# A two-part transformer program on one core: narrow projections made wider, reversed queries, spectra during the down projection, idle transpositions and two reorders

## The reference

```python
def first_block(x, ...):
    n = rms_norm(h, norm1_g)
    mq, mk, mv, gq, gk, gv, g_low, g_out, gate_moba, gate_gla = split(n @ w_in)
    y_moba = softmax(rms(mq) @ rms(mk).T / 8 + t5_bias, causal) @ mv      # 8 heads of 64
    log_a = log_sigmoid(g_low @ gate_up + gate_bias) / 16
    y_gla = rms_norm(gla_attention(gq, gk, gv, log_a)) * silu(g_out)      # 4 heads, chunks of 64
    h = h + (sigmoid(gate_moba) * (y_moba @ w_bm) + sigmoid(gate_gla) * (y_gla @ w_bg)) @ w_out
    h = h + square(relu(rms_norm(h, norm2_g) @ w_up)) @ w_down
def even_layer(x, ...):
    a_val, a_gate, z_a, q, k, v, o, z_b, gates = split(rms_norm(x, g_pre) @ w_in)
    u = depthwise_conv_centred(a_val * sigmoid(a_gate), conv_w, conv_b)   # 31 taps
    y_a = silu(group_layer_norm(u)) * silu(z_a)
    h = mlstm(q, k, v, gates) + reversed mlstm                            # 4 heads
    y_b = sigmoid(o) * rms_norm(h, hn_g) * silu(z_b)
    return x + rms_norm(concat(y_a, y_b) @ w_out, g_post)
def odd_layer(x, ...):
    c_q, c_kv, k_r, f_in, z_c, z_d = split(rms_norm(x, g_pre) @ w_in)
    s = q_nope @ k_nope.T + rope(q_rope) @ rope(k_r).T                    # 8 heads, 128 + 64
    y_c = softmax(s / sqrt(192)) @ v * silu(z_c)
    y_d = (real(fft2(f_in)) @ w_fd) * silu(z_d)
    return x + rms_norm(concat(y_c, y_d) @ w_out, g_post)
```

## Time and profile before

| | us |
|---|---|
| median of 3 runs | 907.76 (906.8 to 912.4) |
| the profiled execution | 908.23 |
| its span | 906.4 |
| TensorE busy | 874.2 (96%) |
| DVE busy | 499.5 (55%) |
| ACT busy | 476.7 (53%) |
| POOL busy | 39.2 (4%) |

### The profile page before, as it was taken

The page is one execution under the profiler, slowest core; times in us unless marked ns, Lnnn a source line. Parts: engine busy times, 40 slices in busy tenths (PEclk is TensorE's granted clock), DMA queues, the critical chain, the costliest instruction groups (busy, mean ns, idle before and its releaser), DMA issues.

```text
span 906.4 us, 10691 instructions
## 1 busy us (share of the span) xinstructions
PE 874.2 (96%) x4015; PEld 704.5 (78%) x4015; DVE 499.5 (55%) x754; ACT 476.7 (53%) x756; POOL 39.2 (4%) x66
## 2 busy tenths in 40 slices
PE   4999999999999999999998999999999899999996
PEld 3888787788888888888885766888888697787685
DVE  4566734555676666435545434856765556555363
ACT  4547644754366555334345364338764567555451
POOL 2100000000000000810000010000000000000000
PEclk9999999999999999999977999999999999999999
DMA  5873445356456565767442414534564547265021
GB/s 178 263 223 120 133 137 140 117 167 206 160 187 191 181 186 186 182 227 252 145 152 80 142 46 161 162 94 163 187 216 154 151 148 253 71 196 164 1 93 47
DMA packets 76579, 141.92 MB, mean 157 GB/s; under 512 B 8489, under 2 KB 10836, under 8 KB 76528
## 3 DMA queue, kind: packets, MB, share of 16 engines
q1 hardware_dynamic: 72432, 134.37, 47.1%
q0 software_dynamic: 4032, 6.86, 2.5%
q10 hardware_dynamic: 64, 0.02, 0.0%
HBM read 140.12 MB, written 2.63 MB: 157 GB/s over the span
## 4 chain that ended last, share of the span: by engine, by line
PE 90%; ACT 4%; DVE 4%; issue 1%; DMA 1%; POOL 0%; DVEq 0%; ACTq 0%; POOLq 0%
PE acc L1518 25%; PE acc L1520 25%; PE acc L1519 25%; PE aux L1547 2%; PE aux L1780 2%; PE aux L1844 1%; PE aux L1969 1%; PE aux L1968 1%; ACT whi L530 1%; PE aux L1959 1%; PE aux L1903 1%; PE aux L1769 1%; DVE wlo L385 1%; DMA vec_in<-in_odd_g_q 1%; PE aux L1646 1%
## 5 line engine op out<-in xcount | busy, mean ns | idle before, releaser
L385 DVE TENSOR_TENSOR wlo<-raw,whi 128x1024 fp32r<-128x1024 f32 (+2 forms) x257 | 304.8, 1203 | 241.4 <-ACT whi L530 240.8
L530 ACT ACTIVATE whi<-raw 128x1024 fp32r<-128x1024 f32 (+2 forms) x257 | 264.9, 1045 | 259.5 <-PE acc L1520 219.6
L1518 PE MATMUL acc<-whi,a_hi 128*128 128x512 f32 (+3 forms) x720 | 284.8, 396 | 3.1 <-DVE wlo L385 1.5
L1520 PE MATMUL acc<-whi,a_lo 128*128 128x512 f32 (+3 forms) x720 | 279.6, 388 | 0.0
L1519 PE MATMUL acc<-wlo,a_hi 128*128 128x512 f32 (+3 forms) x720 | 279.4, 388 | 0.0
L1518 PEld LDWEIGHTS acc<-whi,a_hi 128*128 128x128 f32 x720 | 139.5, 194 | 35.2 <-issue 7.0
L1520 PEld LDWEIGHTS acc<-whi,a_lo 128*128 128x128 f32 x720 | 139.3, 194 | 26.8
L1519 PEld LDWEIGHTS acc<-wlo,a_hi 128*128 128x128 f32 x720 | 139.5, 194 | 26.2 <-issue 0.7
L1518 PE MATMUL acc<-whi,b_hi 128*128 128x512 f32 x234 | 92.4, 395 | 0.1
L1520 PE MATMUL acc<-whi,b_lo 128*128 128x512 f32 x234 | 91.2, 390 | 0.0
L1519 PE MATMUL acc<-wlo,b_hi 128*128 128x512 f32 x234 | 91.1, 389 | 0.0
(11 more groups left out here) (318 smaller groups left out, 765.4 us busy)
## 6 DMA issues: line engine op xcount, KB each, us to landing
raw<-in_even_w_in SPq DMA_DIRECT2D x56, 512.0 KB, 3.8
raw<-in_w_in SPq DMA_DIRECT2D x52, 512.0 KB, 4.2
raw<-in_w_up SPq DMA_DIRECT2D x32, 512.0 KB, 4.5
raw<-in_w_down SPq DMA_DIRECT2D x32, 512.0 KB, 4.5
raw<-in_even_w_out SPq DMA_DIRECT2D x16, 512.0 KB, 3.6
raw<-in_odd_w_in SPq DMA_DIRECT2D x16, 512.0 KB, 4.2
raw<-in_odd_w_out SPq DMA_DIRECT2D x12, 512.0 KB, 4.1
raw<-in_w_branch_gla SPq DMA_DIRECT2D x8, 512.0 KB, 3.4
```

The costliest lines, as they stand in the source:

```text
L385: return e.tensor_tensor(w_view(wlo[u % SPLIT], u), w_view(raw[u % RAW], u), w_view(whi[u % SPLIT], u).bitcast(F32), ALU.subtract)
L530: act.activation(w_view(whi[u % SPLIT], u), w_view(raw[u % RAW], u), ACT.Copy).then_inc(sem("hi_done"), 1)
L1518: pe.matmul(acc_of(c, t), ah[:, ts], hi[:, k], start=first, stop=False)
L1520: ins = pe.matmul(acc_of(c, t), al[:, ts], hi[:, k], start=False, stop=last)
```

## The change

1. norm1's gain is loaded by ACT into n1g_in before all else and transposed by itself; the other vectors are transposed after mq. ACT loads its table first. The one-hot's matmul moves behind mq's first unit.
2. Idle transpositions (`idle_turns`) of the identity: 10 before n1g, 14 before mq, 26 before H's first transposition of the third layer, 10 behind it.
3. Columns 3328 to 3599 of w_in are one chunk, glow, of 272 columns; gv1 keeps 256. In the same way eg has 272 and ew1 256; ACT copies eg's first 256 columns to EZB.
4. Queries are reversed within each tile of 128 when copied out, so that the bias can be read with a stride of +1 from one row; the copy of skew goes. ACT reverses back in PT; the reciprocals are reversed by a product with the matrix flip.
5. gq's and gk's transpositions stand behind the second pt bank.
6. In the o banks both heads' L1686 come first, then both heads' L1692.
7. The taps' spectra are made in dn1, two behind unit 7 and two behind unit 8, and ACT copies them there. gng and gnb are loaded after dn1.
8. The broadcasts mb stand two before eq and two in its middle.
9. KRT is two tiles of 128 rows, one with the lower half zero, one with the upper.

```diff
-        chunk("glow", w_in, 3584, 16, 8, "n1")
+        chunk("glow", w_in, 3328, 272, 8, "n1")
...
-            chunk(name, w_in, n0, 512, 8, "n1")
+            chunk(name, w_in, n0, 256 if name == "gv1" else 512, 8, "n1")
...
-            for name, n0 in [("ea0", 0), ("eg", 7168), ("eb0", 1024), ("ea1", 512), ("eb1", 1536), ("eq", 3072), ("ek", 3584),
+            for name, n0 in [("ea0", 0), ("eg", 6912), ("eb0", 1024), ("ea1", 512), ("eb1", 1536), ("eq", 3072), ("ek", 3584),
...
-                chunk(name, e_in, n0, 16 if name == "eg" else 512, 8, "en")
+                chunk(name, e_in, n0, {"eg": 272, "ew1": 256}.get(name, 512), 8, "en")
...
+            chain(pool.memset(flip[:, :], 0.0))
+            pool.affine_select(out=flip[:, :], in_=flip[:, :], compare_op=ALU.not_equal, fill=1.0, base=1 - P,
+                               pattern=[[1, P]], channel_multiplier=1).then_inc(sem("flip"), 1)
...
-            one = bass.AP(tensor=A["skew"].tensor, offset=A["skew"].offset, ap=[[512 * P, 8], [0, P - 1], [1, 384]])
-            pool.dma_start(A["skew"][:, 1:P, 0:384], one).then_inc(sem("skew_out"), 16)
-            pool.wait_ge(sem("skew_out"), 16)
...
-                src = bass.AP(tensor=A["skew"].tensor, offset=A["skew"].offset + 512 * P * a + P - 1,
-                              ap=[[511, P], [1024 * P, 4], [1, TOK]])
+                src = bass.AP(tensor=A["skew"].tensor, offset=A["skew"].offset + 512 * P * a,
+                              ap=[[1, P], [1024 * P, 4], [1, TOK]])
...
+                pool.wait_ge(sem("units_used"), CH[CI["dn1"]]["units"][-1] + 1)
                 pool.dma_start(gng[:, :], A["even_gn_g_2"][0].partition_broadcast(P)).then_inc(sem("gn_in"), 16)
...
+            act.dma_start(n1g_in[:, :], A["norm1_g"][0].rearrange("(r c) -> r c", c=P)).then_inc(sem("n1g_in"), 16)
+            use("natural_log_exp_and_others")
...
-                copy_out("glow", gl[:, t], t, scale=rms(0, t))
+                acc_wait(act, "glow", t)
+                act.activation(GV[:, t, 768:1024], acc_of("glow", t)[:, 0:256], ACT.Copy, scale=rms(0, t))
+                acc_free(act.activation(gl[:, t], acc_of("glow", t)[:, 256:272], ACT.Copy, scale=rms(0, t)), "glow")
...
-                aux_free(act.activation(flat(PT[:, 4 * i:4 * i + 4]), bank(("pt", i))[:, :], ACT.Copy), ("pt", i))
+                aux_free(act.activation(PT[:, 4 * i:4 * i + 4, ::-1],
+                                        bank(("pt", i))[:, :].rearrange("p (k q) -> p k q", k=4), ACT.Copy), ("pt", i))
...
+                pump("dn1", -5)
                 for n in range(2):
                     key = ("ws", 0, n)
...
+                pump("eg")
+                for t in range(NT):
+                    acc_wait(act, "eg", t)
+                    act.activation(EZB[:, t], acc_of("eg", t)[:, 0:256], ACT.Copy, scale=rms(2, t)
+                                   ).then_inc(sem("zb_copied"), 1)
...
-                        copy_out(f"ew{n}", ETMP[:, t], t, ACT.Silu, rms(2, t))
+                        if n == 0:
+                            copy_out("ew0", ETMP[:, t], t, ACT.Silu, rms(2, t))
+                        else:
+                            use(TABLES[ACT.Silu])
+                            act.activation(ETMP[:, t, 256:512], EZB[:, t], ACT.Silu)
+                            copy_out("ew1", ETMP[:, t, 0:256], t, ACT.Silu, rms(2, t))
...
-                aux_free(dve.tensor_copy(KRT[:, :], bank(("krT",))[:, 0:TOK]), ("krT",))
+                for p in range(2):
+                    own, other = slice(64 * p, 64 * p + 64), slice(64 - 64 * p, 128 - 64 * p)
+                    dve.memset(KRT[other, p], 0.0)
+                    ins = dve.tensor_copy(KRT[own, p], bank(("krT",))[own, 0:TOK])
+                aux_free(ins, ("krT",))
...
+            def idle_turns(b, n):
+
+                for _ in range(n):
+                    pe.transpose(b[:, 0:P], ident[:, :], ident[:, :])
...
-            pe.wait_ge(sem("vec_in"), 16 * (len(VEC_LOADS[0::2]) + 4))
-            pe.wait_ge(sem("vec_in_pool"), 16 * len(VEC_LOADS[1::2]))
-            b = take(("vec",))
-            give(pe.transpose(b[:, 0:P], vec_in[:, :], ident[:, :]), ("vec",))
+            idle_turns(acc[3], 10)
+            pe.wait_ge(sem("n1g_in"), 16)
+            b = take(("n1g",))
+            give(pe.transpose(b[:, 0:8], n1g_in[:, :], ident[0:8, 0:8]), ("n1g",))
...
+            idle_turns(acc[3], 14)
+            product("mq", 0, 1)
             pe.wait_ge(sem("t5_in"), 32)
...
-            product("mq")
+            product("mq", 1, 4)
...
-            product("dn1", 0, 15)
+            product("dn1", 0, 7)
+            if STAGES >= 2:
+                pe.wait_ge(sem("wcv_in"), 48)
+                for w in range(2):
+                    for n in range(2):
+                        b = take(("ws", w, n))
+                        give(pe.matmul(b[:, :], FW[:, w, 1::2], wcv_in[:, 512 * n:512 * n + 512], start=True, stop=True),
+                             ("ws", w, n))
+                    product("dn1", 7 + w, 8 + w)
+            product("dn1", 9, 15)
...
-                product("eq")
+                    if h % 2:
+                        product("eq", h - 1, h + 1)
...
-                pe.wait_ge(sem("h_out"), 2)
-                turn("on", range(4), cols(H))
+                def first_added(b):
+                    idle_turns(b, 26)
+                    pe.wait_ge(sem("h_out"), 2)
+
+                turn("on", range(4), cols(H), first_added)
+                idle_turns(acc_of("okv", 0), 10)
...
-                        ins = pe.matmul(b[:, o:o + TOK], QRT[rows, h // 2, P * t:P * t + P], KRT[rows, :],
+                        ins = pe.matmul(b[:, o:o + TOK], QRT[:, h // 2, P * t:P * t + P], KRT[:, h % 2],
```

More of the change, by code:

```diff
@@ L139, in split_keys @@
             return [("tr", name, j) for j in range((kts + 1) // 2)]
-        AUX = [("vec",)] + split_keys("n1", 8) + [("bias",)]
+        AUX = [("n1g",)] + split_keys("n1", 8) + [("bias",), ("vec",)]
         AUX += [("qkT", w, j) for w in range(2) for j in range(2)]
@@ L144, in program @@
         AUX += [("gz", 0), ("gz", 1)]
-        AUX += [("pt", i) for i in range(6)]
-        AUX += [("gqT", 0), ("gqT", 1), ("gkT", 0), ("gkT", 1)]
-        AUX += [("pv", 0), ("pv", 1), ("kdt", 0), ("kdt", 1), ("ga", 0), ("ga", 1)]
+        AUX += [("pt", 0), ("pt", 1), ("gqT", 0), ("gqT", 1), ("gkT", 0), ("gkT", 1)]
+        AUX += [("pt", i) for i in range(2, 6)]
+        AUX += [("prc",), ("pv", 0), ("pv", 1), ("kdt", 0), ("kdt", 1), ("ga", 0), ("ga", 1)]
         AUX += [("kv", j, i) for j in range(3) for i in range(2)]
@@ L254, in program @@
             ETMP = sb("ETMP", [P, NT, 512], c=c3)
+            gng, gnb = sb("gng", [P, D], c=c3), sb("gnb", [P, D], c=c3)
             WS = sb("WS", [P, 2, D], c=c3)
             SOB = sb("SOB", [P, NT, D], c=c3)
-            gng, gnb = sb("gng", [P, D], c=c3), sb("gnb", [P, D], c=c3)
+            EZB = sb("EZB", [P, NT, 256], c=c3)
             gates = sb("gates", [P, NT, 2, 2, 4], c=c3)
@@ L583, in _ @@
             act.wait_ge(sem("consts"), 1)
+            aux_done(act, ("n1g",))
+            split_hi("n1", range(4), lambda k: n1g[:, k:k + 1])
+            pump("mq", -3)
+            split_hi("n1", range(4, 8), lambda k: n1g[:, k:k + 1])
+            pump("mq", 0)
             for n in range(2):
                 act.wait_ge(sem(f"x_in{n}"), 16)
[L586 to L590, removed]
             norm_stats(0, lambda t: None)
@@ L621, in _ @@
                 copy_out("gk", GQK[:, 1, t], t, scale=rms(0, t))
+            aux_done(act, ("vec",))
             for j in range(2):
@@ L702, in _ @@
             pump("dn0")
+            if STAGES >= 2:
+                pump("dn1", -5)
+                for n in range(2):
+                    key = ("ws", 0, n)
+                    aux_wait(act, key)
+                    aux_free(act.activation(WS[:, 0, 512 * n:512 * n + 512], bank(key)[:, :], ACT.Copy, scale=64.0), key)
+                for n in range(2):
+                    key = ("ws", 1, n)
+                    aux_wait(act, key)
+                    for a in range(2):
+                        rows = slice(64 * a, 64 * a + 64)
+                        ins = act.activation(WS[rows, 1, 512 * n:512 * n + 512], bank(key)[rows, :], ACT.Copy,
+                                             scale=(-64.0, 64.0)[a])
+                    aux_free(ins, key)
             pump("dn1", 3)
@@ L986, in _ @@
             chain(dve.memset(rmask[:, :].rearrange("p (c e) -> p c e", e=64)[:, :, 0:1], 0.0))
-            aux_wait(dve, ("vec",))
-            aux_free(dve.tensor_copy(vec[:, :], bank(("vec",))[:, 0:P]), ("vec",))
-            split_lo("n1", range(4), lambda k: gain("norm1", k))
+            aux_wait(dve, ("n1g",))
+            aux_free(dve.tensor_copy(n1g[:, :], bank(("n1g",))[:, 0:8]), ("n1g",))
+            split_lo("n1", range(4), lambda k: n1g[:, k:k + 1])
             pump("mq", -3)
```

(23 more changed lines are left out.)

69 lines of the change are left out of this document (35 added, 34 removed).

## The result

The changed kernel takes 871.19 us, the median of four runs (869.05 to 873.07), against 907.56 for the kernel before in the same session (906.8 to 912.4). The ratio is 0.9595, with a 95% interval of 0.9555 to 0.9635. The forecast was 869.5 with a range of 864 to 879.

A forecast was written before the change was run, and what follows sets the result against it. TensorE, busy 96% of the span, was taken to bound the kernel. Its terms summed to 38.5 us off the profiled 908.2, giving 869.7; with the median 0.4 lower, it said 869.5, range 864 to 879.

The forecast's parts named there:

- the line through 512 and 320: Matmul start distances, 0.227 us at 512 columns and 0.147 at 320, continued to 0.127 at 272 and 0.120 at 256.
- The start: Up to the first QKN transposition: first product at 10.9 us, 6.8 earlier, half the clock loss kept; net gain 6.3.
- The o banks: Regrouped matmuls drop two of four stationary-width changes in each of four banks, 8 x 0.1: gain 0.8 us.
- Broadcasts in eq: Broadcasts in two pairs shorten sparse stretches, saving half clock of 1.6 us less a restart of 0.4: gain 1.0.
- The heads: KRT padded to 128 rows: 3.5 us per two heads instead of 4.9, gain 5.6.
- 0.7 less cover per head: In the heads, the softmax's way through DVE and ACT gets 0.7 less cover per head; no wait was charged.
- The PT banks: Around the probabilities: the 2.2 us wait for ACT's PT copies stays, now at gkT's bank; gain 0.
- The down projection: Down projection to convolution: 53.2 us becomes 37.2, less 4.3 for spectra moved into dn1; gain 11.7.
- Supply: Rival: ACT and DVE supply takes back 5 to 10 us of narrow-chunk savings at gv1, ew1 and eg; chance 0.18.
- Idle transpositions: Rival: at the start and after the post-norm they don't hold the clock; 5.1 us worse, 875; chance 0.10.
- Full-height loads: Rival: in the heads, 128-row weight loads don't hide, adding up to 3.5 us instead of giving 5.6; 879; chance 0.03.
- The narrow chunks: Rival: 272- and 256-column products leave the fast rate, 0.43 us per matmul instead of 0.12; 929; chance 0.02.

The follow-up runs named there:

- the last kernel: Changed kernel with gv1's first two units and go0's first unit moved into the PT waits, and the broadcasts placed one by one: 867.58 us, ratio 0.9555.
- two units moved: Changed kernel with gv1's first unit ahead of gk's transpositions and its second between the fourth and fifth PT bank: 866.65 us.
- wide chunks: Changed kernel with glow and eg at 16 columns again, gv1 and ew1 at 512: 888.24 us.

## Why the prediction was right

**The reading of the profile held.** Eight of ten terms came within 0.6, because they were counted in distances of starts from windows of one shape. 272 and 256 columns take what the line through 512 and 320 said: 48 matmuls of 272 in 6.11 (6.1 predicted), 48 of 256 in 5.84 (5.8 predicted). That the sum is off by only 0.3 is in part luck: +0.9 at the start and +0.6 at the o banks stand against -1.4 at the broadcasts and -0.4 at the heads.

**The start, 6.3 against 7.2.** The first product stood at 10.68 (predicted 10.9). The stretch from there, 34.12, is 1.4 above 144 x 0.227, where I had put 1.3 for the bias matmul, the vec transposition and the restarts. The larger error is the clock: I counted half of 1.6 as kept, since 2 us stay empty after the idle transpositions. The whole was kept, here and in nine more of the eleven profiled executions that have them; in the last kernel's it was not. No run undoes the early load of norm1's gain: that it is what brings the first product forward by 7.0 is read from the 11.1 us of waiting that are gone and from the first weight unit, behind which the first product now comes. Over the twelve profiled executions of this study the first product came between 9.96 and 11.96, 2.4 after the first unit's landing, and that landing moved between 7.57 and 9.56. Once, with two units moved, it was 2.75: the 14 idle transpositions took 2.8 us instead of 1.7 and held the first product back by 0.35.

**The o banks, 0.8 against 1.4.** The step "two of four changes go, 8 x 0.1" was mis-sized: over the whole stage 40 instructions went from 0.239 to 0.205 each. The eight changes that go each slowed both instructions of a matmul, not one: in the kernel before such a pair took 0.58 us into 64 columns and 0.63 back into 128, and 0.43 where the width stayed. Four of each make 1.4.

**Broadcasts in eq, 1.0 against -0.4.** The mechanism, shorter sparse stretches hold the clock, holds in five of ten profiled executions, then with 1.2 gained, which is the 1.6 - 0.4 of the prediction's own two sizes, where it wrote 1.0. In four half clock comes inside eq, behind the first pair or the second, where it costs as much as before and the second restart on top; in the tenth it comes behind both. The term has more than one value, and I gave one number.

**The heads, 5.6 against 5.2.** The 3.5 per two heads was right; the 0.4 is the wait on ZT that the shorter scores uncovered, which I had named ("0.7 less cover per head") and not charged.

**The PT banks, 0 against -0.2.** The wait kept its size as predicted, at gk's bank. What I missed is that DVE's gk copies then stand between TensorE and the last two PT banks, 1.1 us. The clock stayed up in this execution (1.00 against 0.79), and it gained nothing, since copies set the stage.

**The down projection, 11.7.** Both halves were near, 16.2 less behind and 4.5 more in front (16.0 and 4.3 predicted).

**The rivals.** Supply took nothing back (wide chunks undo exactly what narrow ones gave). Idle transpositions held the clock, but for one start in eleven. Full-height loads cost nothing: 16 instructions in 3.47 where the prediction took 3.5. The narrow chunks stayed on the fast rate.

## What to carry to other kernels

Price an edit to a TensorE-bound kernel by the distance between starts in a window of one shape, and check each stage's end: where copies of another engine set it, neither reordering nor the clock changes anything, but a ready product moved into the wait is free as long as it doesn't hold up what the copies feed (one unit, 2.9 us of products, gave 2.9 here; three, 8.5 us of them, gave 4.1). Fill gaps with work, or where there is none with transpositions, because half clock follows a gap and costs again: 2.5 and 2.2 us here, behind waits of 4.3 and 3.5. Look at several executions before giving a number to a stage at the edge of the clock.

## What the runs showed of the hardware

- fp32 instructions whose rows alternate between 64 and 128 took 0.31 each at 256 columns, and 0.216 when all had 128 rows, half of them zeros in every second matmul: doubling those rows saved a third of the time. 64 rows behind 64 rows of the same half took 0.216 too. Changes between 128 and 64 stationary columns cost alike: the two instructions at a change took 0.58 or 0.63, against 0.43.
- A wait of 3.6 us among the spectra was followed by 10.2 us at half clock, in the rest of the spectra and in ea1; an empty 4.3 us at the start by 6.8 us of it, and the 3.5 behind the post-norm by 6.8. Transpositions in the latter two kept the clock at 1.00, except for the start of one profiled execution in eleven, which met 3.4 us of it behind 2.2 empty ones.
- The same code met half clock at eq in half of the profiled executions, 1.6 us for each stretch. Of ten executions of the changed kernel, the five with a mean granted clock of 0.996 to 0.998 have spans of 867.3 to 868.9 us, the five with 0.992 to 0.993 spans of 870.3 to 871.3: the scatter goes with the clock.
